# The self products of the HGRN2 layer: turned on TensorE and summed on VectorE

## The reference, cut to what matters

```python
def step(state, xs):                      # one chunk of a head
    g_cum = jnp.cumsum(gb, axis=2)
    rel = g_cum[:, :, :, None, :] - g_cum[:, :, None, :, :]
    decay = jnp.exp(jnp.where(incl, rel, -jnp.inf))
    scores = jnp.einsum('bhtd,bhsd,bhtsd->bhts', qb, kb, decay)
    o_intra = jnp.einsum('bhts,bhsv->bhtv', scores, ib)
    o_inter = jnp.einsum('bhtd,bhdv->bhtv', qb * jnp.exp(g_cum), state)
    ...
```

## Time and profile before

| | us |
|---|---|
| Runs of the kernel | 1241.66, 1238.97, 1241.84 |
| Median | 1241.66 |
| The profiled execution | 1240.26 |
| Its span, from first to last instruction | 1238.6 |
| PE busy | 1200.7 |
| DVE busy | 767.2 |
| ACT busy | 421.6 |
| POOL busy | 168.7 |

### The profile page before, as it was taken

One profiled execution on the slowest core, in us unless ns is written; L12 is line 12 of the kernel. 1 busy time (PEld: TensorE's weight loads), 2 busy tenths in 40 slices (PEclk: granted clock), 3 DMA queues, 4 the chain that ended last, 5 costly groups with the idle time before them and its releaser, 6 DMA issues. The chain is left out here.

```text
span 1238.6 us, 20727 instructions
## 1 busy us (share of the span) xinstructions
PE 1200.7 (97%) x7424; PEld 1099.6 (89%) x7424; DVE 767.2 (62%) x1544; ACT 421.6 (34%) x904; POOL 168.7 (14%) x346
## 2 busy tenths in 40 slices
PE   5999999999999999989989999999999999998998
PEld 5999999999999999878868999999899999897787
DVE  4657485857575767644444676777577777667321
ACT  4545353535353545432232122223222322221210
POOL 2322221212121212100019000000000000000000
PEclk9999999999999999999999999999999999997999
DMA  8210223232312200176522112232323230007542
GB/s 230 60 52 18 69 86 103 85 105 76 105 64 79 67 18 1 48 288 208 177 79 68 35 34 67 89 102 86 96 93 102 86 103 18 17 2 268 197 156 93
DMA packets 112655, 115.56 MB, mean 93 GB/s; under 512 B 6832, under 2 KB 88752, under 8 KB 112560
## 3 DMA queue, kind: packets, MB, share of 16 engines
q1 hardware_dynamic: 112560, 114.32, 28.9%
HBM read 80.75 MB, written 33.55 MB: 92 GB/s over the span
## 5 line engine op out<-in xcount | busy, mean ns | idle before, releaser
L29 PE MATMUL p_proj<-w_qkv_hi,ut_hi 128*128 128x384 f32 x512 | 175.8, 343 | 5.2 <-DVE w_qkv_lo L669 4.3
L31 PE MATMUL p_proj<-w_qkv_hi,ut_lo 128*128 128x384 f32 x512 | 172.4, 337 | 0.0
L30 PE MATMUL p_proj<-w_qkv_lo,ut_hi 128*128 128x384 f32 x512 | 172.1, 336 | 0.0
L29 PE MATMUL p_proj<-g_w_ig_hi,next_hi 128*128 128x256 f32 x512 | 147.2, 288 | 0.0
L31 PE MATMUL p_proj<-g_w_ig_hi,next_lo 128*128 128x256 f32 x512 | 144.4, 282 | 0.0
L30 PE MATMUL p_proj<-g_w_ig_lo,next_hi 128*128 128x256 f32 x512 | 143.9, 281 | 0.0
L29 PE MATMUL p_proj<-next_hi,w_qf_hi 128*128 128x512 f32 x320 | 129.7, 405 | 4.8 <-issue 3.0
L31 PE MATMUL p_proj<-next_hi,w_qf_lo 128*128 128x512 f32 x320 | 126.5, 395 | 0.0
L30 PE MATMUL p_proj<-next_lo,w_qf_hi 128*128 128x512 f32 x320 | 126.3, 395 | 0.0
L699 DVE TENSOR_TENSOR_SCAN a_skip<-a_skip 128x128 f32<-128x128 f32 (+3 forms) x64 | 87.3, 1364 | 33.3 <-ACT a_beta L570 31.2
L29 PEld LDWEIGHTS p_proj<-w_qkv_hi,ut_hi 128*128 128x128 f32 x512 | 96.8, 189 | 6.4 <-issue 4.7
(11 more groups left out here) (185 smaller groups left out, 2738.3 us busy)
## 6 DMA issues: line engine op xcount, KB each, us to landing
stage<-in_sb_w_in_dram SPq DMA_DIRECT2D x32, 512.0 KB, 5.9
stage<-in_hg_w_in_dram SPq DMA_DIRECT2D x32, 512.0 KB, 4.7
w_out_hi_scratch<-m_in SPq DMA_DIRECT2D x32, 256.0 KB, 2.1
w_out_lo_scratch<-m_in SPq DMA_DIRECT2D x32, 256.0 KB, 2.3
m_in<-mixed_scratch SPq DMA_DIRECT2D x12, 512.0 KB, 5.7
a_beta<-in_x_dram SPq DMA_DIRECT2D x8, 512.0 KB, 3.6
mixed_scratch<-a_gated SPq DMA_DIRECT2D x8, 512.0 KB, 3.4
m_in<-in_sb_w_out_dram SPq DMA_DIRECT2D x16, 256.0 KB, 3.2
```

The lines of the kernel that those rows point to most:

```text
L29: pe.matmul(out, w_hi, m_hi, start=start, stop=False, skip_group_check=True)
L30: pe.matmul(out, w_hi, m_lo, start=False, stop=False, skip_group_check=True)
L31: return pe.matmul(out, w_lo, m_hi, start=False, stop=stop, skip_group_check=True)
```

## The change

The self products are no longer matmuls. PE turns each tile of `qk` with the identity into `p_misc[2]` and `p_misc[3]`, token on the partition; DVE sums each bank of four tiles along the row with a `tensor_reduce` (128x4x128 to 128x4) into `self_score`. The column of ones goes. `self_done` and `self_ready` are raised twice a head instead of once. PE's wait for `out_ready` moves from ahead of the updates to ahead of the new turns; its wait for `level_placed` there goes; ahead of the updates it now waits for `self_ready`. Level 1 of the next head waits for `level_placed` where it waited for `self_ready`. And only 7 of the 8 tiles of `k_chunk` are turned and copied, as only 7 are used.

```diff
-            "ones_col": sb("ones_col", [P, 1]),
...
-                            act.activation(k_turned[:, 4 * u:4 * u + 4, :], p_misc[u][:, :, :],
+                            act.activation(k_turned[:, 4 * u:4 * u + 4 - u, :], p_misc[u][:, 0:4 - u, :],
...
-                    dve.wait_ge(self_done, h)
+                    dve.wait_ge(self_done, 2 * h)
...
-                dve.wait_ge(self_ready, h + 1)
+                dve.wait_ge(self_ready, 2 * h + 2)
...
                     if mixes and i == 4:
-                        dve.wait_ge(self_done, h + 1)
                         if not known_first(h):
                             dve.wait_ge(o_ready, TILES * h)
-                        dve.tensor_copy(self_score[:, :], p_level[1][:, 0:TILES]).then_inc(self_ready, 1)
+                        for u in range(2):
+                            dve.wait_ge(self_done, 2 * h + u + 1)
+                            dve.tensor_reduce(self_score[:, 4 * u:4 * u + 4], p_misc[2 + u][:, :, :], AX.X,
+                                              ALU.add).then_inc(self_ready, 1)
...
                 elif level == 1 and not known_first(h):
-                    pe.wait_ge(self_ready, h)
+                    pe.wait_ge(level_placed, MASKED * h)
...
                         for u in range(2):
-                            for m in range(4):
+                            for m in range(4 - u):
                                 last = pe.transpose(p_misc[u][:, m, :],
...
                         pe.wait_ge(chunk_ready, h + 1)
-                        pe.wait_ge(level_placed, MASKED * h + (MASKED if projects else 4))
-                        for m in range(TILES):
-                            last = pe.matmul(p_level[1][:, m:m + 1], qk[:, m * P:(m + 1) * P],
-                                             c["ones_col"][:, :], start=True, stop=True)
-                        last.then_inc(self_done, 1)
+                        if not known_first(h):
+                            pe.wait_ge(out_ready, 2 * h)
+                        for u in range(2):
+                            for m in range(4):
+                                last = pe.transpose(p_misc[2 + u][:, m, :],
+                                                    qk[:, (4 * u + m) * P:(4 * u + m + 1) * P], c["ident"][:, :])
+                            last.then_inc(self_done, 1)
...
                     if mixes and i == 4:
-                        if not known_first(h):
-                            pe.wait_ge(out_ready, 2 * h)
                         for u in range(2):
+                            pe.wait_ge(self_ready, 2 * h + u + 1)
                             pe.wait_ge(k_turned_ready, 2 * h + u + 1)
```

More of the change, by code:

```diff
@@ L7 @@
 ACT = mybir.ActivationFunctionType
+AX = mybir.AxisListType
 F32 = mybir.dt.float32
@@ L836, in _ @@
             pool.memset(c["minus_one"][:, :], -1.0)
-            pool.memset(c["head_eps"][:, :], RMS_EPS * P)
-            pool.memset(c["ones_col"][:, :], 1.0).then_inc(pool_made, 1)
+            pool.memset(c["head_eps"][:, :], RMS_EPS * P).then_inc(pool_made, 1)
             for i in range(2):
```

## The result

The changed kernel ran in 1228.96 us (median of 1229.08, 1228.84, 1225.57 and 1230.91), before in 1241.74: a ratio of 0.9906, 95% interval 0.9893 to 0.9918, thus 10 to 13 us less. The prediction had the direction, but about half of the size: 6.0 us less, 1234.7 us, range 1231.4 to 1239.5. The result lies under the range.

The account below looks back on a forecast made before the run. PE, 97% busy, was taken as the bound through heads 0 to 6. Spared there 6.65 us, last head 0.2 gained and 0.85 lost to the clock: 6.0 us off 1240.7 gives 1234.7 us, range 1231.4 to 1239.5.

Parts of the forecast that it names:

- What PE is spared by the turns: Heads 0 to 6: 15 turns replace 7 turns' worth more of PE time, sparing 0.95 us a head, 6.65 us in all.
- What DVE gets: Each head: two sums out of PSUM at 0.65 us replace a 0.16 us copy, 1.14 us more for DVE.
- Rival 3: DVE becomes the bound in step 4 and PE waits for the sums; 1241 us, chance 0.05 together with rival 4.
- The waits that move: Heads 0 to 6: the earlier `out_ready` wait and the changed waits for placements cost nothing.
- The last head: Updates wait for the first sum, PE idles about 1 us before line 29; 0.2 us gained, 0.85 lost to the clock.
- tiles that move in memory: Tiles move when the column of ones goes; no row prices it, a little added to the chance of slower.
- Rival 1: Most of the gain handed back through low clock in and around the last head, 3.4 us; 1237.2 us, chance 0.14.
- Rival 2: In each of seven heads the granted clock falls behind the 15 turns, 1.7 us lost each; 1246 us, chance 0.05.
- Rival 4: A turn of `qk` costs two records as a product does, sparing 0.8 us; 1240 us, chance 0.05 together with rival 3.

Follow-up runs that it names:

- the change alone: Changed kernel with a spare 4-byte tile where the column of ones was, so every tile lies as in the kernel before: 1232.63 us, ratio 0.9932.
- the repeat: The changed kernel run once more, nothing altered, for a second trace: 1226.64 us, ratio 0.9892 against the kernel before.
- the shift alone: Kernel before with the column of ones allocated behind all other second-layer tiles, so tiles between move 32 bytes down: 1235.0 us, ratio 0.995.
- that of 128 bytes: Changed kernel with the second layer's left tiles 128 bytes above their places in the kernel before: 1227.0 us, ratio 0.9896.

## Why the prediction was wrong, by its own steps

**What PE is spared by the turns: right, a little low.** Predicted 0.95 us a head, found 1.02 in the trace after and 1.04 from the change alone. The last turns of a row cost PE less than 0.109: 0.80 us for eight, the lower of the two prices I had. Seven heads: 7.2 us for 6.65.

**What DVE gets: right.** 0.64 us a sum for 0.65. Idle time ahead of its gate product 0.44 for 0.50, no PE wait on DVE in step 4, as said. Rival 3 is out.

**The waits that move: right,** nothing waited for `out_ready` or for the placements in heads 0 to 6.

**The last head: the mechanism right, the cost unproven.** The new wait (0.93) and the idle time ahead of the output products came in the trace after, 1.96 for about 1; the repeat has no such idle time. I had taken the transfer's end as fixed. From the turns of head 6's outputs to line 121 it is 15.6 to 17.7 us in the fourteen traces, 16.2 to 17.0 in those without the turns, so the idle time hangs on it more than on the change. I charged 0.85 us for the clock less 0.2 gained. From the turns of head 6's outputs to head 7's last output product, the starts give 25.8, 24.8, 25.1 and 26.3 us in the four traces without the turns, mean 25.5, and 24.1 to 27.8 in the nine with single turns, mean 25.7. So the change costs 0.2 us here, less than the spread; the loss at half clock occurs (1.9 us above), in the trace after it did not.

**The failed step: tiles that move in memory,** for which the prediction "added a little" to a chance and nothing to the sum. Measured, it is 0.48 us a head: the 192 products of 256 columns run 2.2 ns faster each, 0.42 us, and the 96 of 512 columns, both of whose tiles lie on the right side, about 0.8 ns (22.10 us of PE in head 4 before, 22.02 with the shift alone). With the first projection, which has no mixing beside it, that makes 7 x 0.48 + 0.46 = 3.8 us. I had all that was needed to ask: the diff takes a tile away ahead of all others, and 288 products a head, 192 of them with 256 columns, bind PE. No row of before gives the price, but the range should have held something for it: what was measured later, 2.2 ns on each of 1536 products, is 3.4 us. With 3.8 us more spared the forecast would have been 1230.9, under its own range.

**The sum as it should have been:** 7.2 + 3.8 - 0.2 = 10.8 us, against 11.7 measured by the ratio (10.2 to 13.3) and 13.4 in the repeat (11.4 to 15.5). The rest is at least in part the stretch at half clock behind the idle time of 3 us ahead of head 3. The prediction knew it, feared a second one, and left it in the sum as it was; that it could go was put at nothing. It is in ten of fourteen traces, among them both of before, and in neither of the changed kernel. There head 3 came 61.55 and 61.13 us behind head 2, before 64.58 and 64.23; less a head each, 3.35 and 2.93 stand against 4.87 and 4.51, so about 1.6 us. The idle time itself is alike (3.0 and 2.7 before, 3.1 and 2.7 after). It doesn't take the turns to miss the stretch, for the shift alone misses it too; and the kernel with the turns made twice, whose tiles lie as in the changed one, has it. The fourth trace without it is that of 128 bytes. Whether the changed kernel misses it by a habit of its timing or by luck stays open.

**Rival 1** (gain handed back) did not come. The "rather sparse work" on which it leaned was none: PE was busy for 6.81 of the 7.00 us. **Rival 2**, the clock falling behind the turns, did not come with 15 turns in a row, nor with 23. **Rival 4** is out: eight turns of `qk` show as 8 records. For this the Trainium skill ("TensorE: Matmul & The Clock Gate", Part 4: PE-mode transpose) gave the reason, that turns do not count as work for the clock in the same way. Between dense projections nothing of it shows here: 1.00 in both rows. Ahead of head 3 eight turns and the idle time stand together in front of the stretch at half clock, so no run here tells what the turns have to do with that one.

## What to carry to other kernels

When PE is the bound and runs back to back, price a product by its weights as well as by its columns: eight float32 products against a single column held PE for 1.7 us, eight turns for 0.8. When a diff adds or drops a tile ahead of others, compare PE's time for products that the edit leaves alone; and before believing a gain or a loss of 0.3%, put a spare tile in its place and run that. Where the same two tiles feed thousands of products, try some distances between them: here 96 bytes up held PE for 5.54 us for 48 products, where the changed kernel had 5.73. And compare whole times, for a faster product can be paid for elsewhere.

## What the runs showed of the hardware

The spacing of these products with 256 moving columns (float32 in the profile, type F32R in the kernel, one record each) depends on the distance between the stationary and the moving tile in the on-chip memory. Six distances 32 bytes apart gave 114.9 to 120.0 ns, not in order; moving the left side 32 bytes up or the right side 32 down gave the same value; with the two moving tiles alone at +96 bytes and the rest at +256 it was 113.7. In the first layer 256-column products between other tiles stand 113 ns apart in the mean. The 96 products of 512 columns in head 4, whose two tiles lie both on the right side, moved by 1.4 ns each at most (21.96 to 22.10 us together in all traces). The cause in the hardware isn't shown: no run tells whether the weights or the moving columns come later.
